# A hybrid decoder layer on one core: other amounts of filler work between the mixer steps, and earlier mixer loads on SP's queue

## The reference

```python
hn = _rmsnorm(x, p['norm_pre_mix'])
z = jnp.einsum('btd,dp->btp', hn, p['w_in'])
(z_lx, z_lg, z_gu, z_gv, z_rw, z_mx, z_mv, z_mo, z_mi, z_mf, z_gate) = _split(z, PROJ_SIZES)
y_a, lru_buf, lru_h = _rglru_branch(z_lx, z_lg, lru_buf, lru_h, p, is_start)
y_b, gm_v = _gmlp_branch(z_gu, z_gv, p)
y_c, rw_shift, rw_S = _rwkv7_branch(z_rw, rw_shift, rw_S, p)
y_d, ml_buf, ml_C, ml_n, ml_m = _mlstm_branch(z_mx, z_mv, z_mo, z_mi, z_mf, ml_buf, ml_C, ml_n, ml_m, p)
br = jnp.einsum('btnc,ncd->btnd', jnp.stack([y_a, y_b, y_c, y_d], axis=2), p['w_branch'])
merged = jnp.sum(jax.nn.sigmoid(z_gate.reshape(Bx, T, N_BRANCH, D_MODEL)) * br, axis=2)
x = x + _rmsnorm(jnp.einsum('btd,de->bte', merged, p['w_out']), p['norm_post_mix'])
g, u = jnp.split(jnp.einsum('btd,df->btf', _rmsnorm(x, p['norm_pre_ffn']), p['w_ff_in']), 2, axis=-1)
x = x + _rmsnorm(jnp.einsum('btf,fd->btd', jax.nn.silu(g) * u, p['w_ff_out']), p['norm_post_ffn'])
```

## Time and profile before

| | |
|---|---|
| median of 3 runs | 2212.21 us (2211.4 to 2216.17) |
| the profiled execution's own time | 2216.17 us |
| its span in the trace | 2214.4 us |
| TensorE busy | 2136.8 us, 96% |
| DVE, ACT, POOL busy | 734.3, 747.2 and 1433.8 us |
| granted TensorE clock, mean over the span | 0.974 |
| chain that ended last | PE 41%, POOL 29%, issue 28% |

### The profile page before, as it was taken

How to read it: one execution, slowest core, us unless ns; L and a number is a source line. 1 busy time by engine, 2 the same in 40 slices (tenths; PEclk the granted TensorE clock), 3 DMA queues, 4 the chain that set the end, 5 groups by cost and what they waited for, 6 DMA issues and landing times.

```text
span 2214.4 us, 39904 instructions
## 1 busy us (share of the span) xinstructions
PE 2136.8 (96%) x15845; PEld 2078.3 (94%) x15845; DVE 734.3 (33%) x1129; ACT 747.2 (34%) x879; POOL 1433.8 (65%) x1100
## 2 busy tenths in 40 slices
PE   6999999999999999999999699999999999999995
PEld 6988999989999998999999599999999999999995
DVE  4556444386423223416633711111000111111223
ACT  4353333334322221343333333333333333333331
POOL 5764845566844443778877177777777777777773
PEclk9999999999999998999999699999999999999997
DMA  6644644444633332468654144444555545444552
GB/s 213 200 163 151 197 146 156 154 148 135 186 114 120 112 120 79 136 188 283 223 198 145 46 152 149 146 150 147 149 152 148 155 148 148 150 148 148 148 149 84
DMA packets 116325, 336.74 MB, mean 152 GB/s; under 512 B 14197, under 2 KB 43229, under 8 KB 115586
## 3 DMA queue, kind: packets, MB, share of 16 engines
q1 hardware_dynamic: 99282, 313.18, 45.6%
q10 hardware_dynamic: 16944, 22.15, 2.7%
HBM read 311.41 MB, written 23.88 MB: 151 GB/s over the span
## 4 chain that ended last, share of the span: by engine, by line
PE 41%; POOL 29%; issue 28%; DVE 1%; POOLq 0%; ACT 0%; DVEq 0%
POOL w_lo L1346 29%; PE bank L1366 14%; PE bank L1367 14%; PE bank L1368 14%; DVE mix L1853 0%; DVE xres L1856 0%; POOLq L1340 0%; POOLq L1344 0%; DVE rstd L1723 0%; PE bank L1379 0%; POOLq L1346 0%; ACT rstd L1585 0%; DVE ssum L1790 0%; DVE term L1787 0%; DVE mix L1842 0%
## 5 line engine op out<-in xcount | busy, mean ns | idle before, releaser
L1346 POOL TENSOR_TENSOR w_lo<-w_raw,w_hi 128x512 fp32r<-128x512 f32 (+1 forms) x1096 | 1433.6, 1334 | 746.6 <-ACT w_hi L1642 367.0
L1366 PE MATMUL bank<-x_hi,w_hi 128*128 128x320 f32 x3360 | 1064.8, 317 | 44.1 <-POOL w_lo L1346 35.8
L1368 PE MATMUL bank<-x_hi,w_lo 128*128 128x320 f32 x3360 | 1049.1, 312 | 0.0
L1367 PE MATMUL bank<-x_lo,w_hi 128*128 128x320 f32 x3360 | 1049.0, 312 | 0.0
L1366 PEld LDWEIGHTS bank<-x_hi,w_hi 128*128 128x128 f32 x3360 | 640.8, 191 | 61.2 <-issue 41.1
L1367 PEld LDWEIGHTS bank<-x_lo,w_hi 128*128 128x128 f32 x3360 | 641.6, 191 | 1.4
L1368 PEld LDWEIGHTS bank<-x_hi,w_lo 128*128 128x128 f32 x3360 | 640.9, 191 | 0.0
L1567 ACT ACTIVATE w_hi<-w_raw 128x1024 fp32r<-128x1024 f32 (+1 forms) x329 | 340.2, 1036 | 419.1 <-PE bank L1368 394.3
L1642 ACT ACTIVATE w_hi<-w_raw 128x1024 fp32r<-128x1024 f32 x180 | 188.7, 1057 | 463.0 <-PE bank L1368 412.8
L1366 PE MATMUL bank<-a_hi,w_hi 128*128 128x320 f32 x704 | 217.4, 309 | 0.0
L1368 PE MATMUL bank<-a_hi,w_lo 128*128 128x320 f32 x704 | 217.4, 309 | 0.0
(11 more groups left out here) (324 smaller groups left out, 1394.3 us busy)
## 6 DMA issues: line engine op xcount, KB each, us to landing
w_raw<-in_w_f SPq DMA_DIRECT2D x212, 512.0 KB, 4.0
w_raw<-in_w_fi SPq DMA_DIRECT2D x176, 512.0 KB, 3.8
w_raw<-in_w_fo SPq DMA_DIRECT2D x64, 512.0 KB, 3.5
front_scratch<-ev ACTq DMA_DIRECT2D x106, 160.0 KB, 2.4
w_raw<-in_w_br SPq DMA_DIRECT2D x32, 512.0 KB, 4.8
w_raw<-in_w_o SPq DMA_DIRECT2D x32, 512.0 KB, 3.8
arena<-front_scratch SPq DMA_DIRECT2D x24, 640.0 KB, 5.8
w_raw<-in_w_fo SPq DMA_DIRECT2D x32, 384.0 KB, 3.2
```

The lines of the kernel that those rows point to most:

```text
L1346: low = nc.gpsimd.tensor_tensor(w_lo[:, q % RING, c0:c1], w_raw[:, q % RING, c0:c1], w_hi[:, q % RING, c0:c1].bitcast(F32), ALU.subtract)
L1366: pe.matmul(out, wh, hi[:, k0 + k, :], start=first and k == 0, stop=False)
L1367: pe.matmul(out, wh, lo[:, k0 + k, :], start=False, stop=False)
L1368: mm = pe.matmul(out, wl, hi[:, k0 + k, :], start=False, stop=last and k == tiles - 1)
```

## The change

Fill sizes: A_conv 9 to 8, D_rows 9 to 12, D_conv 14 to 12, C_kk 5 to 4, C_scaled 14 to 17. With them `at` becomes 24, 30 (A_tail), 33 (B_in), 49 (D_rows), 61 (D_conv), 105 (C_low), 112 (C_kk), 117 (C_rk), 134 (C_scaled) and again 196 at the end. `stored` issues three weight loads fewer before it waits. On ACT the Gelu of `a_gz` goes ahead of A's gates and the Sigmoid of `d_o` ahead of the heads; DVE's wait for the latter moves ahead of the heads too. DVE has a new point inside A's convolution, other points in D, and makes kk after all three token mixings.

```diff
@@ stored
-            part[sp](2 * block + 5 + AFTER)
+            part[sp](2 * block + 2 + AFTER)
@@ mixers_pe
-            fill("A_conv", 9)
+            fill("A_conv", 8)
-            fill("D_rows", 9)
+            fill("D_rows", 12)
-            fill("D_conv", 14)
+            fill("D_conv", 12)
-            fill("C_kk", 5)
+            fill("C_kk", 4)
-            fill("C_scaled", 14)
+            fill("C_scaled", 17)
@@ mixers_act
             sc.activation(a_t[:, 1, :], a_t[:, 0, :], ACT.Exp, scale=-1.0).then_inc(S("A_exp"), 1)
+            act.wait_ge(S("A_gz_in"), 16)
+            sc.activation(a_gz, a_gz, ACT.Gelu_apprx_tanh).then_inc(S("A_gelu"), 1)
             for c in range(C4):
                 full(act, "A_r", c)
@@
             upto(act, "A_tail", 1)
-            act.wait_ge(S("A_gz_in"), 16)
-            sc.activation(a_gz, a_gz, ACT.Gelu_apprx_tanh).then_inc(S("A_gelu"), 1)
@@
-            upto(act, "D_rows", 8)
+            upto(act, "D_rows", 4)
             act.wait_ge(S("D_abs"), 1)
@@
-            upto(act, "D_rows", 1)
+            upto(act, "D_rows")
             act.wait_ge(S("D_bm"), 2)
@@
             sc.activation(d_c, d_c, ACT.Silu).then_inc(S("D_silu"), 1)
+            act.wait_ge(S("D_o_in"), 16)
+            sc.activation(d_o, d_o, ACT.Sigmoid).then_inc(S("D_osig"), 1)
@@ (in the heads, h == 0)
-                if h == 0:
-                    act.wait_ge(S("D_o_in"), 16)
-                    sc.activation(d_o, d_o, ACT.Sigmoid).then_inc(S("D_osig"), 1)
@@ mixers_dve
             conv_pads(a_cin, a_xc[:, :, 0:64], a_st, O("lconv"))
+            upto(dve, "A_conv", 3)
             conv(a_cin, a_acc, a_xc, "cw_l", "cb_l", "A_conv")
@@
-            upto(dve, "D_rows", 8)
+            upto(dve, "D_rows", 4)
             dve.wait_ge(S("D_exp"), 1)
             softplus_of(rf, r4, r2, r3, r5, r6, 1)
-            upto(dve, "D_rows", 4)
+            upto(dve, "D_rows", 2)
@@
-            upto(dve, "D_conv", 10)
+            upto(dve, "D_conv", 8)
@@
             dve.wait_ge(S("D_silu"), 1)
+            dve.wait_ge(S("D_osig"), 1)
@@ (in the heads, before D_y)
-                dve.wait_ge(S("D_osig"), 1)
@@ (inside the loop over k, r, v)
-                if x == 1:
-                    link(tt(c_kk, c_k, vb4("kk"), ALU.mult)); sync()
-                    put(tt(c_rk, c_kk, c_kk, ALU.mult), "C_kk_sq", 1)
@@ (after that loop)
+            upto(dve, "C_kk", 2)
+            link(tt(c_kk, c_k, vb4("kk"), ALU.mult)); sync()
+            put(tt(c_rk, c_kk, c_kk, ALU.mult), "C_kk_sq", 1)
```

More of the change, by code:

```diff
@@ L1141, in mix_in @@
                 put(tt(z, z, d, ALU.add), name, 1)
-            vb4 = lambda name: bc(V(name, 0, 4), 2, T)
             dve.wait_ge(S("D_out"), 128)
@@ L1157, in mixers_dve @@
                        f"C_mixed_{name}")
-                if x == 1:
-                    link(tt(c_kk, c_k, vb4("kk"), ALU.mult)); sync()
-                    put(tt(c_rk, c_kk, c_kk, ALU.mult), "C_kk_sq", 1)
+            vb4 = lambda name: bc(V(name, 0, 4), 2, T)
+            upto(dve, "C_kk", 2)
+            link(tt(c_kk, c_k, vb4("kk"), ALU.mult)); sync()
+            put(tt(c_rk, c_kk, c_kk, ALU.mult), "C_kk_sq", 1)
             for h in range(4):
```

## The result

The changed kernel takes 2251.38 us (median of 4 runs, 2247.43 to 2253.3), the kernel before, run beside it, 2214.19 us. The ratio is 1.0163, 95% interval 1.0149 to 1.0176: slower by 37 us. The forecast was 2248, 36 us above the median of before that it started from. The profiled execution took 2251.57 us, its span is 2249.8 us against 2214.4, and the granted clock over the span is 0.968 against 0.974.

A forecast was written before the change was run, and what follows sets the result against it. TensorE, busy 96% of the span, was taken as the bound: its fixed work plus its waits. New waits of 27.9 us and 8 of slow clock, together 36, gave 2248 us for the median; range 2222 to 2264.

The forecast's parts named there:

- The SP edit at D_silu: At D_silu: ACT's split of piece 63 stands behind a late weight load; TensorE waits 7.5 us (4 to 9).
- D_rows: TensorE waits before the transposes of L442, as the chain on ACT and DVE starts later: 11 us (5.5 to 15).
- the second part: The part of DVE's chain to D_rows after the softplus, 12.6 us before, shrinks to about 5.
- rival 1: Weight loads behind SP's wait are early enough; D_rows waits 6.4 us, total about 2231; chance 0.18.
- A_conv with the Gelu: A's gates wait 2.9 us (2 to 6) for the convolution; piece 19, behind the Gelu, 1.5 (0 to 3).
- the B terms: In B: piece 29 lands late, 0.5 us (0 to 3); wss load starts later, 1 us (0 to 1).
- rival 2: Earlier mixer loads on SP's queue end existing waits; new D_rows and D_silu waits within 17 us; about 2195; chance 0.08.
- C_rk: TensorE reaches the C_rk wait one piece sooner, its chain starting as before: 3.5 us more (2.5 to 4.5).
- At nothing: C_scaled, D_conv, ACT's second D_rows point and the Sigmoid of d_o were given no cost.
- Piece 102: The existing TensorE wait for POOL's low half there, 4.1 us, was given no change.
- The clock: Four waits are long enough to bring the slow clock behind them, 2 us each: 8 us.

The follow-up runs named there:

- run 3: D's fill counts and points alone (D_rows 11, D_conv 12, points moved as in the change), on the kernel before: 2222.98 us, ratio 1.004.
- run 7: The changed kernel with D's points back at pieces 39 and 43, all twelve pieces of cover kept: 2237.21 us, ratio 1.0101.
- run 2: The changed kernel with the SP edit undone from block 11 on: 2240.33 us, ratio 1.0112.
- run 5: A_conv 8 instead of 9 with the DVE point inside the convolution, D_rows 10, on the kernel before: 2225.21 us, ratio 1.0051.
- run 6: The Gelu of a_gz ahead of A's gates, with the shorter loads-ahead for blocks 3 and 7, on the kernel before: 2220.01 us, ratio 1.0029.
- run 4: C's edits alone (C_kk 4, C_scaled 17, kk behind the three mixings), on the kernel before: 2216.8 us, ratio 1.0012.
- run 1: The SP edit alone (weight loads up to piece 2b+6 instead of 2b+9 ahead of each store wait), on the kernel before: 2220.56 us, ratio 1.0023.

## Why the prediction came out, point by point

- **The SP edit at D_silu.** Predicted 7.5 (4 to 9), measured 5.94, and 5.92 with the edit alone. The mechanism was right, the term too large: I took 9.7 us from the group to the landing of the next weight load, and it was 7.4 (288.76 to 296.12). The wait lies within the bounds.
- **D_rows.** Predicted 11 (5.5 to 15), measured 12.0. I had the Exp end 14.0 us after piece 42 and it was 12.8; the softplus with the evacuation 13.7 and it was 13.6; the second part 5 and it was 6.7, as two instructions still ran into POOL; and TensorE's arrival 21.5, where six pieces are 21.1. The two durations from which I read the second part, 1.14 and 0.16 us, do not show by themselves what I took from them, for both instructions ran while POOL was busy. Others do: L1033, L1037 and L1038 took 1.09, 1.18 and 1.24 us before, and 0.15, 0.15 and 0.18 in the changed kernel, beside an idle POOL. Runs 3 and 7 show that the points cause it, run 2 what the late split adds. This also tells rival 1 apart: its 6.4 at D_rows is what run 2 shows with the loads in time, 6.49. In the changed kernel they were not in time.
- **A_conv with the Gelu.** Predicted 2.9 and 1.5, measured 5.2 and 0.98. This is the mis-sized term: I costed the two edits one by one, and the Gelu's bunch of splits put POOL beside the whole convolution. Run 5 has 3.5 without it, run 6 has 2.6 without the shorter cover. The upper bound of 6 held for this reason ("POOL is more continuously busy beside it"), but I had not traced it to the Gelu.
- **B.** I gave the B terms 1.5 us of loss. The wait at the normalised v went from 1.87 to 2.3, which looks like a small cost and is the sum of two larger ones: 4.7 for the shorter cover and a later chain (6.56 in run 2, without the edit), 4.25 gained by the SP edit. I had reckoned the wss load 1 us later "against its chain", and it came 2.9 us sooner than in run 2 and landed faster. Its order against the weight loads decided, as rival 2 has it, though for one wait of 4 us and not for 17.
- **C_rk.** Predicted 3.5 more, measured 3.0 more (4.1), and 2.6 in run 4.
- **At nothing.** C_scaled, D_conv and the Sigmoid show no wait in the changed kernel, as argued.
- **Piece 102.** I left it at 4.1 and it was 2.14. That kk leaves POOL's way there I had not seen; how much of the 1.9 is that and how much spread, run 4 leaves open.
- **The clock.** The listed waits up to the last mixer rose by 25.2 us (27.9 predicted, with piece 102 unchanged), the span by 35.4, so some 10 us are left for slow clock, where I had 8. TensorE's busy time, 9.7 us more for the same matmuls, says the same. That the slow clock followed four waits is in the windows above. The split into waits and clock is read from one execution each.

Taken one by one (runs 1, 3, 4, 5 and 6) the parts cost 6.3, 8.7, 2.5, 11.1 and 5.9 us, 34.5 in sum, against 37 together. That nearness is partly luck: runs 1 and 6 both hold the earlier loads of blocks 3 and 7; at D_rows the parts reinforce one another (12.0 from 6.5 and nothing), at B they cancel.

The 3 us too much in the waits and the 2 us too little in the clock nearly cancel too, so the forecast is nearer than its terms are. Of the 3 us by which the time passed the forecast, 2 are the base: the kernel before took 2214.19 us beside the changed one, and 2212.21 when I wrote.

## What to carry to other kernels

Where filler work hides a chain, count the cover from the point at which the chain may start, and not from the last place that TensorE met: list for every engine what stands ahead of the chain's first instruction. D_rows got three pieces more of filler and a start six pieces later (45 for 39), and waited. At A's gates and at C_rk, where the start stayed, one piece less showed at once (3.5 and 2.6 us in runs 5 and 4). On an engine that issues two streams in order, an edit that lets one go earlier makes the other late. Look at who stands, in order, behind each transfer that is delayed, and check whether the same edit is what another place needed. And before a wait is attacked, look at the slack of the next one: two of the three waits removed here came back in full within 40 us.

## What the runs showed of the hardware

VectorE beside a busy GpSimd is slowed even in instructions with one tensor input: the 128x256 COPY took 1.42 us instead of 0.29, the 128x12 COPY 1.15 instead of 0.17, the four 128x344 TENSOR_SCALAR 5.1 us in the changed kernel and 3.5 before. The 4x320 scan of L1030 took 1.80 us in the kernel before, with POOL busy beside it, and 0.81 in the changed kernel, with POOL idle. The Trainium skill ("SBUF — State Buffer", section "Who interferes with whom") names copies and tensor_scalar among those that can take the shared ports, and the trace agrees.

From the first pad to the end of the convolution DVE needed 17.0 us before and 19.6 in run 6, where the same pieces' subtractions came in one unbroken run of 21.5 us. Whether the missing pauses cost this or the amount is not shown: POOL was busy for 12.1 us of that stretch before and for 14.7 in run 6.
